# Third phase of a decoder step: output projection as plain fp32 matmuls of whole values in place of three products of high and low parts

## The chip, the cores and the metric

The kernel runs on one core of one Trainium2 chip. The time is the device time of the whole program in microseconds; of the kernel before there are three runs, median 2069.62 us (2069.22 to 2070.6). Times inside the program come from one profiled execution. Its span, from the first to the last instruction, is 2068.6 us, and its own time is 2070.4 us, 1.8 us more.

## The reference

One layer of a decoder with two parallel branches (latent attention and causal pooling), gated, merged, projected and added to the input, then a final norm. All is fp32; there are 2048 prompt tokens and 8 decoded ones. The change is in the last lines:

```python
merged = jax.nn.sigmoid(g_att) * y_att + jax.nn.sigmoid(g_pool) * y_pool
x = x + merged @ w_out                    # (2056 x 1024) @ (1024 x 1024)
...
y_prompt = rmsnorm(xp, g_final)
y_sample = rmsnorm(xs, g_final)
```

## The kernel before, in words

The program is one stream of instructions for each engine, tied by semaphores. First come the latent projections and attention, then the part called `merge`, whose tiles begin with `d_` in the profile. It has three phases. Phase one makes the gates (tiles `d_wr` with `d_ht` or `d_hb`), phase two the two branch projections and their gated sum (`d_wr` with `d_gat` or `d_gpl`; the sum is stored as `out_mg`), phase three multiplies the sum by `w_out`.

Nearly every large product is made of **high and low parts**. ScalarE copies an fp32 tile into one of type fp32r, which rounds it (the high part). VectorE subtracts that from the source (`split`, L91 to L93; the profile puts it down to L93) and has the low part, also fp32r. `three_products` (L127 to L134, the matmul is on L131) then issues three matmuls for each slice k of the contraction: high by high, high by low, low by high.

Phase three splits `w_out` and each group of 256 tokens into two by two quarters and uses a scheme of seven products in place of eight (Strassen's, in the form with 15 additions). Its moving operands are the seven quarters or sums of quarters of the weights, 28 tiles `moved[m]` of 128 x 2 x 512 (parts, columns); its stationary ones are the seven of the tokens, `kept[g % 2][k][part]`, 128 x 7 x 128 each. The quarters are staged in `d_staged` (loads on SP's queue, L2041 to L2052; sums on GpSimd, L2433 to L2444), and split by ScalarE (L2270) and VectorE (`low_staged`, L2542). The weights are split by L2255, L2260 and L2532 to L2540; the last ten of the 28 come late, as `d_raw`.

The order of work is the table `JOIN` (L1750 to L1764). A step (g, p) is product p of group g: four slices k, accumulated in one bank of PSUM over 512 columns. There are 8 groups x 7 products = 56 steps, in the order (0,1) (0,2) (0,6) (0,5) (0,7) and then for each group g: (g,1) (g-1,4) (g-1,3) (g,2) (g,6) (g,5) (g,7). Two more steps with g = 8 are the eight decoded tokens (`tail_product`, L2761), with a stationary of 8 columns, 20 slices together. TensorE's step (g,1) waits for the split tokens of the group (`kept_ok`, L2784); after each step ScalarE copies or VectorE adds the result out of PSUM and counts up `evicted` or `added`. At the end come the sum of squares (ScalarE), the factor (GpSimd, `rms`), the scaling (VectorE) and the store.

Two places elsewhere in the kernel issue matmuls on tiles of type f32, that is, plain fp32 ones:

```python
for hh in range(4):        # L627, inside "for a in range(2)", "for k in range(KQ)": 16 calls
    head = 4 * a + hh
    mm = pe.matmul(ps_q[2 * a + k][:, hh * R:hh * R + R], wuq_t[:, head, k * P:k * P + P],
                   wuk_t[:, head, :], start=True, stop=True)
...
for s, j, to in columns(g):   # L1670, four calls, eight times in all: 32 calls
    pe.matmul(ps_s[n % 2][to, :], qd[:, 0, s, :], ckeys[:, n % 2, j, :], start=True, stop=False)
```

The second has stationaries of 32 columns that write to four different groups of 32 partitions (`to`). L1674, right behind it, is of the same kind with 256 moving columns; L1683 has a stationary of 128 columns and 8 moving ones.

Of the kernel before, what the change touches and what calls it, by code (L numbers as in the profile page):

```python
# [20 lines left out]
f32 = mybir.dt.float32  # L21
# [3 lines left out]
ACT = mybir.ActivationFunctionType  # L25
# [55 lines left out]
HD = KD // 2  # L81
# [45 lines left out]
def three_products(pe, out, stationary, moving, depth, first=True, last=True, again=False):  # L127

    for k in range(depth):
        for a, b in ((0, 0), (0, 1), (1, 0)):  # L130
            mm = pe.matmul(out, stationary(a, k), moving(b, k),  # L131
                           start=first and k == 0 and a + b == 0,
                           stop=last and k == depth - 1 and a == 1, skip_group_check=again)
    return mm  # L134
# [1633 lines left out]
MOVED_OF = {1: 0, 2: 1, 6: 2, 5: 3, 7: 4, 4: 5, 3: 6}  # L1768
KEPT_OF = {1: 0, 2: 1, 4: 2, 5: 3, 6: 4, 7: 5, 3: 6}
# [21 lines left out]
def merge(nc, io, keep, ahead):  # L1791
# [6 lines left out]
    with ExitStack() as ctx:  # L1798
        def at(first, name, shape, dt=f32):
            return nc.alloc_sbuf_tensor_at("d_" + name, shape, dt, offset=first)  # L1800

        def sem(name):
# [20 lines left out]
        first = where["scores"]  # L1823
# [3 lines left out]
        out = [at(out_at + n * row, f"out{n}", [P, TA]) for n in range(4)]  # L1827
# [36 lines left out]
        moved = [at(first, f"moved{n}", [P, 2, HALF], f32r) for n, first in enumerate(wide_at)]  # L1864
        quarters = at(wide_at[0], "quarters", [P, 4, HALF])
        changed = at(wide_at[2], "changed", [P, 4, HALF])
        moved_f = [at(where["gap"] + n * piece, f"moved_f{n}", [P, HALF]) for n in range(2)]
        raw_at = {m: t_at[0] + (n * piece if n < 3 else 8 * NH * T - (len(RAW_ORDER) - n) * piece)
                  for n, m in enumerate(RAW_ORDER)}
        raw = {m: at(first, f"raw{m}", [P, HALF]) for m, first in raw_at.items()}  # L1870
# [8 lines left out]
        kept = [[[at(kept_at[2 * i + a], f"kept0_{i}_{a}", [P, 7, P], f32r) for a in range(2)] for i in range(HD)],  # L1879
                [[at(t_at[0] + (2 * i + a) * 3584, f"kept1_{i}_{a}", [P, 7, P], f32r) for a in range(2)]  # L1880
                 for i in range(HD)]]
# [8 lines left out]
        tail_f = at(staged_at[1], "tail_f", [P, KD, TAIL_C])  # L1890
        tail = at(staged_at[1] + 256, "tail", [P, 2, KD, TAIL_C], f32r)
# [3 lines left out]
        w_in, w_hi, w_ok, unit_ok = ahead["w_in"], ahead["w_hi"], ahead["w_ok"], ahead["unit_ok"]  # L1895
# [56 lines left out]
        moved_hi, moved_ok, MOVED_HI, MOVED_OK = const_hi, const_lo, 2, 3  # L1952
        staged_in, STAGED_BASE = ol_in, OL_BASE + 16 * NC * NH // 2
        TURN_BASE = added_t + 4 * HD
        kept_hi, kept_ok, KEPT_BASE = ahead["h_hi"], h_ok, 3 * HD * NAP
# [45 lines left out]
        staged_row = lambda n: staged[n % (2 if n < HD else 3)]  # L2001
# [211 lines left out]
        def _(act):  # L2213
# [38 lines left out]
            def high_moved(m):  # L2252

                act.wait_ge(moved_in[m % 2], MOVED_BASE[m % 2] + 16 * (m // 2 + 1))
                act.activation(moved[m][:, 0, :], moved_f[m % 2][:, :], ACT.Copy).then_inc(moved_hi, 1)  # L2255

            def high_raw(m):

                act.wait_ge(raw_in, RAW_BASE + 16 * len(RAW_ORDER))
                act.activation(moved[m][:, 0, :], raw[m][:, :], ACT.Copy).then_inc(moved_hi, 1)  # L2260

            def high_staged(q, i):

                n = HD * q + i
                if n == 1:
                    act.wait_ge(gp_lo, NC)
                if n == HD:
                    act.wait_ge(moved_ok, MOVED_OK + NMOVED)
                act.wait_ge(t_ok, TURN_BASE + 4 * n + 4)
                act.activation(kept[q % 2][i][0][:, :, :], staged_row(n)[:, 1:8, :], ACT.Copy).then_inc(kept_hi, 1)  # L2270

            def squares(q):

                act.wait_ge(added, add_join[q, 3])
                if q >= 2:
                    act.wait_ge(rinv_ok, 3 * (q - 1))
                for t in range(2):
                    for part in range(2):
                        n = 4 * q + 2 * t + part
                        wait(act, ss_ok, n - 2)  # L2280
                        act.activation(bank[JUNK_BANK[n % 3]][:, :], y[q % 2][t][:, part * HALF:part * HALF + HALF], ACT.Square,
                                       accum_out=stat[:, q % 2, part, t:t + 1]).then_inc(ss_ok, 1)

            for s, (g, p) in enumerate(SLOTS):
# [22 lines left out]
                if p == 4 and g + 1 - POOLED in pool_groups:  # L2307
                    n = pool_at(g + 1 - POOLED)
# [34 lines left out]
            for n, (g, p) in enumerate(JOIN):  # L2343
                act.wait_ge(unit_ok, UNITS + n + 1)
                if g < GROUPS_C:
                    if p == 1:
                        act.wait_ge(*((added, add_join[g - 1, 7]) if g else (m_ok, NC * KD)))
                        act.activation(p1c[:, :], bank[A_BANK[g % 2]][:, :], ACT.Copy).then_inc(evicted, 1)
                    if p == 6:
                        if g:  # L2350
                            act.wait_ge(added, add_join[g - 1, 3])
                        act.activation(u2c[:, :], bank[A_BANK[g % 2]][:, :], ACT.Copy).then_inc(evicted, 1)
                    if p == 7:
                        act.wait_ge(added, add_join[g, 5])
                        act.activation(p1c[:, :], bank[A_BANK[g % 2]][:, :], ACT.Copy).then_inc(evicted, 1)
                for m in JOIN_RAW.get((g, p), ()):
                    high_raw(m)
                for i in JOIN_STAGED.get((g, p), ()):
                    high_staged(pair_of(g, p), i)
                if (g, p) == (GROUPS_C - 1, 6):  # L2360
                    act.wait_ge(staged_in[0], STAGED_BASE + 48 * HD * GROUPS_C // 2 + 16)
                    act.activation(tail[:, 0, :, :], tail_f[:, :, :], ACT.Copy).then_inc(kept_hi, 1)
                if p == 3:
                    squares(g)
            act.wait_ge(added, add_join[GROUPS_C, 2])
            act.wait_ge(rinv_ok, 3 * (GROUPS_C - 1))
            for part in range(2):
                n = 4 * GROUPS_C + part
# [322 lines left out]
        def _(pe):  # L2691
# [10 lines left out]
            for s, (g, p) in enumerate(SLOTS):  # L2702
# [20 lines left out]
                if p == 1 and g - POOL_MM in pool_groups:  # L2723
                    n, pg = pool_at(g - POOL_MM), (g - POOL_MM) % PAIRS
# [4 lines left out]
                    for part in range(2):  # L2729
                        mm = three_products(pe, bank[PM_BANK[part]][:, 0:HA], lambda a, _: wpl[:, a, pg, :],  # L2730
                                            lambda b, _: pool2[:, b, HA * part:HA * part + HA], 1)
# [29 lines left out]
            def tail_product(out, pairs):  # L2761

                for n, (k0, block_of) in enumerate(pairs):
                    mm = three_products(pe, out, lambda a, k: tail[:, a, k0 + k, :],
                                        lambda b, k: moved[HD * block_of + k][:, b, :], HD,
                                        first=n == 0, last=n == len(pairs) - 1)
                mm.then_inc(unit_ok, 1)

            pe.wait_ge(yp_ok, NC * KD)
# [1 line left out]
            for g, p in JOIN:  # L2771
                if g == GROUPS_C:
                    pe.wait_ge(kept_ok, KEPT_BASE + HD * GROUPS_C + 1)
                    if p == 1:
                        pe.wait_ge(added, add_join[GROUPS_C - 1, 2])
                        tail_product(bank[C_BANK][0:TAIL_C, :], ((0, MOVED_OF[1]), (HD, MOVED_OF[2])))
                    else:
                        pe.wait_ge(added, add_join[GROUPS_C - 2, 4])
                        tail_product(bank[A_BANK[0]][0:TAIL_C, :], ((0, MOVED_OF[1]), (0, MOVED_OF[5]), (HD, MOVED_OF[3])))
                    continue  # L2780
                if g == 0:
                    pe.wait_ge(moved_ok, MOVED_OK + {5: HD * MOVED_OF[5] + HD, 7: 18 + 5}.get(p, HD * MOVED_OF[p] + HD))
                if p == 1:
                    pe.wait_ge(kept_ok, KEPT_BASE + HD * g + HD)  # L2784
                    if g >= 2:
                        pe.wait_ge(added, add_join[g - 2, 4])
                if p == 2 and g:
                    pe.wait_ge(added, add_join[g - 1, 2])
                if p in (6, 7):
                    pe.wait_ge(evicted, evict_join[g, 1 if p == 6 else 6])  # L2790
                if p == 4:
                    pe.wait_ge(evicted, evict_join[g, 7])
                if p == 5 and g >= 2:
                    pe.wait_ge(added, add_join[g - 2, 3])
                if p == 3:
                    pe.wait_ge(added, add_join[g, 7])
                to = bank[C_BANK if p == 2 else (B_BANK if p in (5, 3) else A_BANK)[g % 2]][:, :]
                of = kept[g % 2]
                three_products(pe, to, lambda a, k: of[k][a][:, KEPT_OF[p], :],
                               lambda b, k: moved[HD * MOVED_OF[p] + k][:, b, :], HD, first=p in (1, 2, 5),  # L2800
                               again=p in (6, 7, 4, 3)).then_inc(unit_ok, 1)


def finish(outs):
# [184 lines left out]
```

## Time and profile before

| | us |
|---|---|
| median of three runs | 2069.62 |
| profiled execution, its own time | 2070.4 |
| its span | 2068.6 |
| TensorE matmul busy (97% of the span) | 2005.8 |
| VectorE busy | 1498.7 |
| ScalarE busy | 1124.5 |
| GpSimd busy | 523.7 |
| phase three on TensorE, first matmul to last end | 1885.24 to 2061.80 |

Busy time of an engine is the union of its instructions' spans. A matmul's span reaches from its start to its modelled end; the next one starts well before that, so the time that a matmul costs in a dense stretch is the distance from start to start, not the mean duration. It is read from a window: its length divided by the number of instructions that touch it. Weight loads (PEld) are recorded apart and run beside the matmuls. The granted clock is 1.00 at TensorE's upper level of 2.4 GHz and 0.50 at its lower of 1.2 GHz.

### The profile page before, as it was taken

The numbers are of one execution on the slowest core, as the hardware profiler recorded it, in microseconds if no ns is written. First come the engines' busy times: TensorE is split into PE (matmuls) and PEld (weight loads), VectorE is DVE, ScalarE is ACT, GpSimd is POOL, SyncE is SP. The second block draws the span as 40 slices with busy tenths as digits, with TensorE's granted clock in tenths as the row PEclk, the third lists the DMA queues.
The fourth block names the chain that finished last, engine by engine and source line by source line (L and its number), as shares of the span: only waits on it lengthen the run. The fifth ranks groups of instructions, "written<-read, shape, count | busy, mean of one in ns | idle before, by whom it ended". The sixth has DMA issues, their size and how long they took to land.

```text
span 2068.6 us, 37208 instructions
## 1 busy us (share of the span) xinstructions
PE 2005.8 (97%) x13077; PEld 1831.8 (89%) x13077; DVE 1498.7 (72%) x3208; ACT 1124.5 (54%) x2271; POOL 523.7 (25%) x647
## 2 busy tenths in 40 slices
PE   7999999999999999999999999999999989998998
PEld 6999888888888888699999999999999989997885
DVE  7786887887888776568668758767875777675554
ACT  4446765556555555556665665666564434442442
POOL 3444364333211010213004003101111331122451
PEclk9999999999999999999999999999999999999999
DMA  8876465344221032367776776786888988886452
GB/s 302 267 237 187 121 192 168 112 123 125 90 72 31 6 122 92 129 174 224 245 235 206 248 232 194 259 246 195 252 273 255 322 285 296 289 282 192 135 175 84
DMA packets 284249, 396.97 MB, mean 192 GB/s; under 512 B 34016, under 2 KB 152680, under 8 KB 283032
## 3 DMA queue, kind: packets, MB, share of 16 engines
q1 hardware_dynamic: 278272, 374.26, 58.2%
q0 software_dynamic: 2304, 12.58, 1.6%
q10 hardware_dynamic: 3488, 7.75, 1.2%
q8 instruction: 105, 1.72, 0.3%
q14 instruction: 80, 0.66, 0.1%
HBM read 295.77 MB, written 98.96 MB: 191 GB/s over the span
## 4 chain that ended last, share of the span: by engine, by line
PE 40%; DVE 7%; issue 3%; DMA 3%; ACT 2%; POOL 1%; SPq 1%; ACTq 0%; DVEq 0%; POOLq 0%
PE b_ps L131 40%; DVE d_wr L93 3%; ACT d_wr L1345 1%; DMA d_moved_f<-in_w_quarters 1%; DMA d_quarters<-in_w_quarters 1%; DVE d_pool L93 0%; DVE d_pooled L2594 0%; POOL d_ols L93 0%; DMA d_zsf<-out_zs 0%; DVE d_c L2579 0%; DMA d_olf<-out_olat 0%; DVE d_moved L93 0%; DVE d_gat L93 0%; DVE d_out L2508 0%; DMA d_raw<-in_w_quarters 0%
## 5 line engine op out<-in xcount | busy, mean ns | idle before, releaser
L93 DVE TENSOR_TENSOR d_wr<-d_ws,d_wr 128x512 fp32r<-128x512 f32 x568 | 429.4, 762 | 210.3 <-ACT d_wr L1345 204.2
L1345 ACT ACTIVATE d_wr<-d_ws 128x512 fp32r<-128x512 f32 x568 | 350.1, 628 | 247.7 <-PE b_ps L131 239.5
L131 PE MATMUL b_ps<-d_ht,d_wr 128*128 128x258 f32 x3072 | 398.7, 284 | 6.8 <-DVE d_wr L93 5.2
L131 PEld LDWEIGHTS b_ps<-d_ht,d_wr 128*128 128x128 f32 x3072 | 380.2, 189 | 13.4 <-DVE d_wr L93 12.0
L759 PE MATMUL b_ps<-kt,k_qs 128*128 128x512 f32 (+2 forms) x1520 | 337.8, 370 | 1.2 <-DVE b_p L1147 1.1
L131 PE MATMUL b_ps<-d_hb,d_wr 128*128 128x258 f32 x2304 | 302.7, 284 | 6.2 <-DVE d_wr L93 4.6
L759 PEld LDWEIGHTS b_ps<-kt,k_qs 128*128 128x128 f32 x1520 | 265.4, 188 | 48.5 <-DVE b_p L1147 3.9
L131 PEld LDWEIGHTS b_ps<-d_hb,d_wr 128*128 128x128 f32 x2304 | 287.4, 189 | 9.3 <-DVE d_wr L93 7.3
L1101 ACT ACTIVATE b_pt<-b_ps 128x512 fp32r<-128x512 f32 x272 | 158.3, 597 | 167.5 <-PE b_ps L1207 114.0
L93 DVE TENSOR_TENSOR b_pt<-b_ps,b_pt 128x512 fp32r<-128x512 f32 x272 | 182.9, 688 | 87.8 <-ACT b_pt L1101 86.4
L1207 PE MATMUL b_ps<-b_pt,kv 128*128 128x512 f32 x816 | 227.8, 407 | 0.0
L1094 ACT ACTIVATE b_p<-b_p,b_bias 128x1024 f32<-128x1024 f32 (+7 forms) x192 | 171.6, 896 | 60.0 <-DVE b_low L1154 59.1
L131 PE MATMUL b_ps<-d_gat,d_wr 128*128 128x412 f32 x960 | 184.8, 353 | 2.2 <-DVE d_wr L93 2.2
L131 PEld LDWEIGHTS b_ps<-d_gat,d_wr 128*128 128x128 f32 x960 | 181.7, 191 | 4.0 <-DVE d_wr L93 2.9
L131 PE MATMUL b_ps<-d_moved,d_kept 128*128 128x512 f32 x672 | 160.5, 401 | 7.9 <-DVE d_spf L2630 5.6
L1207 PEld LDWEIGHTS b_ps<-b_pt,kv 128*128 128x128 f32 x816 | 143.4, 189 | 24.2
L131 PEld LDWEIGHTS b_ps<-d_moved,d_kept 128*128 128x128 f32 x672 | 129.1, 192 | 39.1 <-DVE d_spf L2630 5.9
L93 POOL TENSOR_TENSOR k_qs<-k_qf,k_qs 128x512 fp32r<-128x512 f32 (+1 forms) x52 | 71.1, 1368 | 359.8 <-issue 203.2
L1198 PE MATMUL b_ps<-ident,b_p 128*128 128x128 f32 x1088 | 149.0, 273 | 3.3 <-DVE b_pt L93 1.6
L1198 PEld LDWEIGHTS b_ps<-ident,b_p 128*128 128x128 f32 x1088 | 128.4, 140 | 25.6 <-DVE b_pt L93 3.3
L1147 DVE TENSOR_SCALAR_CACHE_REDUCE b_p<-b_ps 128x512 f32<-128x512 f32 (+1 forms) x192 | 125.1, 668 | 14.7 <-PE b_ps L759 13.0
L1171 DVE TENSOR_SCALAR b_p<-b_p,b_inverse 128x1024 f32<-128x1024 f32 (+7 forms) x192 | 133.2, 716 | 0.7
(248 smaller groups left out, 2562.9 us busy)
## 6 DMA issues: line engine op xcount, KB each, us to landing
d_ws<-out_w_sums SPq DMA_DIRECT2D x256, 256.0 KB, 3.5
d_ws<-in_w_pairs SPq DMA_DIRECT2D x192, 256.0 KB, 3.1
d_ws<-in_w_last SPq DMA_DIRECT2D x120, 256.0 KB, 4.4
b_quarters<-in_w_pairs SPq DMA_DIRECT2D x16, 1024.0 KB, 8.1
out_w_sums<-b_sums SPq DMA_DIRECT2D x16, 1024.0 KB, 10.3
out_q<-a_qout SPq DMA_DIRECT2D x32, 384.0 KB, 4.0
d_hf<-out_ht SPq DMA_DIRECT2D x32, 258.0 KB, 3.4
out_zs<-d_out SPq DMA_DIRECT2D x32, 258.0 KB, 4.3
```

The costliest lines, as they stand in the source:

```text
L93: return e.tensor_tensor(low, source, high.bitcast(f32), ALU.subtract)
L131: mm = pe.matmul(out, stationary(a, k), moving(b, k), start=first and k == 0 and a + b == 0, stop=last and k == depth - 1 and a == 1, skip ...
L759: mm = pe.matmul(out, qs[:, a, h, :], keep["kt"][:, first:first + size, b, :], start=k == 0, stop=k == len(pairs) - 1)
L1094: act.activation(span, span, ACT.Exp, bias=bias[:, at:at + 1], scale=-1.0 if negated else SCALE, accum_out=total[:, at, part:part + 1]).th ...
L1101: act.activation(pt[n % NPT][:, 0, :], ps_t[n % NTB][:, :], ACT.Copy).then_inc(pt_hi, 1)
L1147: dve.tensor_scalar(out, inp, 1.0, None, ALU.mult, ALU.max, accum_out=top[:, at, c:c + 1]).then_inc(s_sb, 1)
L1171: dve.tensor_scalar(span, span, inverse[:, at:at + 1], None, ALU.mult).then_inc(p_ok, 1)
L1198: mm = pe.transpose(ps_t[n % NTB][:, h * P:h * P + P], weights(u, h, slice(j * P, j * P + P)), ident[:, :])
L1207: mm = pe.matmul(ps_o[u % 2][:, :], kv[:, j, a, :], pt[n % NPT][:, b, :], start=j == 0 and k == 0, stop=j == tiles(u) - 1 and k == 2)
L1345: act.activation(ahead["wr"][s % WR][:, 0, :, :], ahead["ws"][s % WS][:, :, :], ACT.Copy).then_inc(ahead["w_hi"], 1)
```

## The change

In phase three each slice k is one matmul on whole fp32 values instead of three on parts. The tiles keep their places and sizes: `moved[m][:, 0, :]`, `kept[..][0]` and `tail[:, 0]` are now written through `bitcast(f32)`, so that ScalarE's copy does not round, and read through `bitcast(f32)`. VectorE's subtractions, the semaphores and their counts, the loads and the order of the steps are as before; the low tiles are still written but no matmul reads them.

```diff
             def high_moved(m):
-                act.activation(moved[m][:, 0, :], moved_f[m % 2][:, :], ACT.Copy).then_inc(moved_hi, 1)
+                act.activation(moved[m][:, 0, :].bitcast(f32), moved_f[m % 2][:, :], ACT.Copy).then_inc(moved_hi, 1)
...
-                act.activation(kept[q % 2][i][0][:, :, :], staged_row(n)[:, 1:8, :], ACT.Copy).then_inc(kept_hi, 1)
+                act.activation(kept[q % 2][i][0][:, :, :].bitcast(f32), staged_row(n)[:, 1:8, :], ACT.Copy).then_inc(kept_hi, 1)
...
             def tail_product(out, pairs):
                 for n, (k0, block_of) in enumerate(pairs):
-                    mm = three_products(pe, out, lambda a, k: tail[:, a, k0 + k, :],
-                                        lambda b, k: moved[HD * block_of + k][:, b, :], HD,
-                                        first=n == 0, last=n == len(pairs) - 1)
+                    for k in range(HD):
+                        mm = pe.matmul(out, tail[:, 0, k0 + k, :].bitcast(f32),
+                                       moved[HD * block_of + k][:, 0, :].bitcast(f32), start=n == 0 and k == 0,
+                                       stop=n == len(pairs) - 1 and k == HD - 1)
...
-                three_products(pe, to, lambda a, k: of[k][a][:, KEPT_OF[p], :],
-                               lambda b, k: moved[HD * MOVED_OF[p] + k][:, b, :], HD, first=p in (1, 2, 5),
-                               again=p in (6, 7, 4, 3)).then_inc(unit_ok, 1)
+                for k in range(HD):
+                    mm = pe.matmul(to, of[k][0][:, KEPT_OF[p], :].bitcast(f32),
+                                   moved[HD * MOVED_OF[p] + k][:, 0, :].bitcast(f32), start=p in (1, 2, 5) and k == 0,
+                                   stop=k == HD - 1, skip_group_check=p in (6, 7, 4, 3))
+                mm.then_inc(unit_ok, 1)
```

TensorE's program in step (0,1), the first of phase three, before. The names are the moving tile and the stationary one; of `d_kept_k_part` the second number is 0 for the high and 1 for the low part:

```order
L131 MATMUL b_ps<-d_moved_13099,d_kept_0_0_13142 128x512 [waits d_const_lo,d_h_ok,d_ya_ok,d_yp_ok]
L131 MATMUL b_ps<-d_moved_13099,d_kept_0_0_13142 128x512
L131 MATMUL b_ps<-d_moved_13099,d_kept_0_1_13143 128x512
L131 MATMUL b_ps<-d_moved_13100,d_kept_1_0_13144 128x512 x2
L131 MATMUL b_ps<-d_moved_13100,d_kept_1_1_13145 128x512
L131 MATMUL b_ps<-d_moved_13101,d_kept_2_0_13146 128x512 x2
L131 MATMUL b_ps<-d_moved_13101,d_kept_2_1_13147 128x512
L131 MATMUL b_ps<-d_moved_13102,d_kept_3_0_13148 128x512 x2
L131 MATMUL b_ps<-d_moved_13102,d_kept_3_1_13149 128x512
```

The same place of the changed kernel, with steps (0,2) and (0,6) behind it:

```order
L2801 MATMUL b_ps<-d_moved_13099,d_kept_0_0_13142 128x512 [waits d_const_lo,d_h_ok,d_ya_ok,d_yp_ok]
L2801 MATMUL b_ps<-d_moved_13100,d_kept_1_0_13144 128x512
L2801 MATMUL b_ps<-d_moved_13101,d_kept_2_0_13146 128x512
L2801 MATMUL b_ps<-d_moved_13102,d_kept_3_0_13148 128x512
L2801 MATMUL b_ps<-d_moved_13103,d_kept_0_0_13142 128x512 [waits d_const_lo]
L2801 MATMUL b_ps<-d_moved_13104,d_kept_1_0_13144 128x512
L2801 MATMUL b_ps<-d_moved_13105,d_kept_2_0_13146 128x512
L2801 MATMUL b_ps<-d_moved_13106,d_kept_3_0_13148 128x512
L2801 MATMUL b_ps<-d_moved_13107,d_kept_0_0_13142 128x512 [waits d_evicted,d_const_lo]
```

Twelve matmuls became four, in the same order of slices and behind the same waits. The last step of the program, that of the decoded tokens, was 36 matmuls and is 12:

```order
L131 MATMUL b_ps<-d_moved_13099,d_tail 8x512 [waits d_added,d_h_ok]
L131 MATMUL b_ps<-d_moved_13099,d_tail 8x512 x2
L131 MATMUL b_ps<-d_moved_13100,d_tail 8x512 x3
L131 MATMUL b_ps<-d_moved_13101,d_tail 8x512 x3
L131 MATMUL b_ps<-d_moved_13102,d_tail 8x512 x3
```

```order
L2765 MATMUL b_ps<-d_moved_13099,d_tail 8x512 [waits d_added,d_h_ok]
L2765 MATMUL b_ps<-d_moved_13100,d_tail 8x512
L2765 MATMUL b_ps<-d_moved_13101,d_tail 8x512
L2765 MATMUL b_ps<-d_moved_13102,d_tail 8x512
L2765 MATMUL b_ps<-d_moved_13111,d_tail 8x512
```

What moved is only TensorE's own list; the rows of ScalarE, VectorE, GpSimd and SP are the same in both kernels. A row here is a call in the program, and the trace can hold more than one record for it.

## Rows read from the trace of the kernel before

**Rows 1.** The page: busy tenths and granted clock in 40 slices.
```profile
PE   7999999999999999999999999999999989998998
PEclk9999999999999999999999999999999999999999
```

**Rows 2.** Chain that ended last, from 1885 us: start us, us, what, count.
```profile
1885.24 5.50 PE b_ps L131 x12
...
1890.77 0.60 ACT d_p1c L2348
...
1895.52 1.10 DVE d_kept L93
1896.69 0.03 SPq L2047
...
1897.59 2.57 DMA d_staged<-out_mg
...
1902.10 0.96 ACT d_kept L2270
...
1903.15 1.10 DVE d_kept L93
...
1904.30 157.50 PE b_ps L131 x672
2061.80 0.78 issue
...
2065.10 1.27 DVE d_y_tail L2687
```

**Rows 3.** Windows, matmuls of L131: stretch, length, PE and PEld busy (touching), clock.
```profile
1885.00:1890.97 5.97, 5.73 (x14) 4.47 (x15) 0.50 0.54 133
1890.97:1904.30 13.33, 11.04 (x48) 8.65 (x46) 1.00 0.76 233
1904.30:1908.00 3.70, 3.70 (x9) 2.94 (x10) 0.54 0.62 190
1925.00:2050.00 125.00, 125.00 (x541) 99.00 (x540) 1.00 0.45 143
```

**Rows 4.** Window, all engines: PE, PEld, DVE, ACT, POOL busy, PE clock.
```profile
1925.00:1950.00 25.00, 25.00 (x109) 20.23 (x108) 15.49 (x18) 9.05 (x17) 14.11 (x26) 1.00 0.58 182
```

**Rows 5.** Groups of TensorE by form: busy us, mean ns | idle before, releasers.
```profile
L131 PE MATMUL b_ps<-d_moved,d_kept 128*128 128x512 f32 x672 | 160.5, 401 | 7.9 <-DVE d_spf L2630 5.6 <-DVE d_kept L93 2.3
L131 PE MATMUL b_ps<-d_moved,d_tail 128*8 128x512 f32 x60 | 14.2, 394 | 0.0
L131 PEld LDWEIGHTS b_ps<-d_moved,d_kept 128*128 128x128 f32 x672 | 129.1, 192 | 39.1 <-DVE d_spf L2630 5.9 <-DVE d_kept L93 2.7
```

**Rows 6.** Plain fp32 matmuls by line: duration ns min/median/max, first and last start us.
```profile
L629 PE MATMUL b_ps<-a_wuk_t,a_wuq_t x32: 275/421/582, 8.1 to 14.3; 128*128 128x128 f32 x32
L1671 PE MATMUL b_ps<-c_ckeys,e_qd x64: 588/593/617, 832.0 to 871.8; 128*32 128x512 f32 x64
L1674 PE MATMUL b_ps<-c_rkeys,e_qd x128: 377/379/380, 832.9 to 872.8; 128*32 128x256 f32 x128
L1683 PEld LDWEIGHTS b_ps<-kt,e_qd x16: 190/192/193, 829.4 to 831.1; 128*128 128x128 f32 x16
L1683 PE MATMUL b_ps<-kt,e_qd x16: 175/256/257, 829.5 to 831.1; 128*128 128x8 f32 x16
```

**Rows 7.** Timeline of TensorE in three short windows near 842 us: start, us, what.
```profile
841.76 0.64 PE L1671 MATMUL b_ps<-c_ckeys,e_qd 128*32 128x512 f32 x4
842.22 0.61 PE L1671 MATMUL b_ps<-c_ckeys,e_qd 128*32 128x512 f32 x4
842.64 0.40 PE L1674 MATMUL b_ps<-c_rkeys,e_qd 128*32 128x256 f32 x4
```

**Rows 8.** L629 after 14 us, the part at the upper clock.
```profile
L629 PE MATMUL b_ps<-a_wuk_t,a_wuq_t x6: 275/275/276, 13.7 to 14.3; 128*128 128x128 f32 x6
```

**Rows 9.** Groups of ScalarE that write fp32r and f32: busy us, mean ns.
```profile
L1101 ACT ACTIVATE b_pt<-b_ps 128x512 fp32r<-128x512 f32 x272 | 158.3, 597 | 167.5 <-PE b_ps L1207 114.0 <-PE b_ps L1198 47.7 <-issue 2.2
L2352 ACT ACTIVATE d_u2c<-b_ps 128x512 f32<-128x512 f32 x8 | 4.8, 596 | 3.6 <-PE b_ps L131 3.6
```

More of the change, by code:

```diff
@@ L2254, in high_moved @@
                 act.wait_ge(moved_in[m % 2], MOVED_BASE[m % 2] + 16 * (m // 2 + 1))
-                act.activation(moved[m][:, 0, :], moved_f[m % 2][:, :], ACT.Copy).then_inc(moved_hi, 1)
+                act.activation(moved[m][:, 0, :].bitcast(f32), moved_f[m % 2][:, :], ACT.Copy).then_inc(moved_hi, 1)
             def high_raw(m):
                 act.wait_ge(raw_in, RAW_BASE + 16 * len(RAW_ORDER))
-                act.activation(moved[m][:, 0, :], raw[m][:, :], ACT.Copy).then_inc(moved_hi, 1)
+                act.activation(moved[m][:, 0, :].bitcast(f32), raw[m][:, :], ACT.Copy).then_inc(moved_hi, 1)
             def high_staged(q, i):
@@ L2361, in _ @@
                     act.wait_ge(staged_in[0], STAGED_BASE + 48 * HD * GROUPS_C // 2 + 16)
-                    act.activation(tail[:, 0, :, :], tail_f[:, :, :], ACT.Copy).then_inc(kept_hi, 1)
+                    act.activation(tail[:, 0, :, :].bitcast(f32), tail_f[:, :, :], ACT.Copy).then_inc(kept_hi, 1)
                 if p == 3:
```

## The prediction, made before the changed kernel was run

> **What bounds the kernel now.** I read the page first: TensorE is busy nine tenths or more in nearly every slice and at its upper clock [rows 1]. So a change in TensorE's work shows in the time one to one, if the place that it touches is as dense as the rest. The chain of waits answers that for phase three [rows 2]: from 1904.30 to 2061.80 us it is nothing but matmuls of L131, 157.50 us for 672 of them, and before that it goes once through TensorE (12 matmuls, 5.50 us) and once around it, through the tokens of group 1. The idle time says the same: 5.6 us before the first matmul, 2.3 us before step (1,1), none else [rows 5]. The other engines have room: in a window of 25 us VectorE is busy 15.49, ScalarE 9.05, GpSimd 14.11 [rows 4]. The end behind the last matmul, 6.8 us (2061.80 to 2068.6), is squares, factor and scaling of the decoded tokens, and is not touched.
>
> **The change, part by part.**
>
> *Removed:* 672 + 60 = 732 matmuls on parts [rows 5]. Their cost is the distance from start to start, not the 401 ns of the group row. In the window 1925 to 2050, 541 touch 125.00 us at clock 1.00 [rows 3]; with the last one's duration of about 0.39 added, 125.39 / 541 = 231.8 ns. The pure column time would be 512 / 2.4 GHz = 213 ns, so each bears some 18 ns of surcharge. The chain agrees: (157.50 - 1.6 for a piece at the lower clock - 0.2) / 672 = 231.7.
>
> *Added:* 56 x 4 + 20 = 244 calls on whole values. Three things must be known of one: how many records it is, how long each holds TensorE, and whether the weight load hides.
> Records: L629 stands in the program as 16 calls and L1671 as 32, and the trace has 32 and 64 [rows 6]. So a plain fp32 call is two matmuls, and 244 calls are 488 records.
> Time of one: L1671 has our 512 columns, L1674 256, both at the upper clock; their durations are 593 and 379 [rows 6]. The difference, 214 ns for 256 columns, is 0.836 ns a column, two cycles of 2.4 GHz; 512 columns are 428 ns. The starts agree: four L1671 at 841.76 (side by side, in four column groups), their second records at 842.22, L1674 at 842.64 [rows 7], steps of 0.46 and 0.42, 0.44 in the mean. These stationaries are 32 columns wide and ours are 128. For that there is L629 with 128: six records from 13.7 to 14.3 at duration 275 [rows 8], about 0.11 apart for 128 columns, again two cycles a column with at most a few ns on top. So I take 0.430 us a record, 0.860 a call, against 3 x 0.2318 = 0.695 before. Bounds: 0.42 from below (the shortest step of the row); from above 2 x 0.2318 = 0.464, if each of the two cycles per column bears the surcharge of a whole pass before.
> Weight loads: 192 ns for 128 columns of plain fp32, by L1683 [rows 6], as for the parts [rows 5]. Each would lie beside a matmul of 430, where it now lies beside one of 232. I cost it at nothing. If it were not covered, L1683, whose 8 columns hide nothing, prices it: 16 records from 829.5 to 831.1, 0.107 each.
>
> The Trainium skill has a rule here, in "FP8 and Floating Point Precision", TensorE Precision Notes: true FP32 takes four passes through the array. By column time alone four passes are 4 x 213 = 853 ns a call, which is what the two records of two cycles a column give; the trace would show them folded in pairs. Read as four passes each as dear as one before, it gives the upper bound above, and is a rival below.
>
> *The start of the phase.* Here something is given back. Before, the clock was at 0.50 until 1890.97 [rows 3], after the idle 5.6 us; it should be again, since nothing ahead of 1885.24 changes. Plain records then take 0.86: (1890.97 - 1885.24) / 0.86 = 6.7 of them by the time the clock rises. Step (0,1) has 8, so the last starts at about 1891.1 and ends at 1891.7, where it ended at 1890.74 before. The first five steps are 40 records: 33.3 more at 0.43 is 14.3 us, and TensorE is ready for step (1,1) at 1905.3. What it waits for there are the split tokens of group 1. Their chain starts at the end of step (0,1): ScalarE's copy, the last weights, VectorE's splits, SP's load, 2.57 us of transfer, sums, ScalarE, VectorE, ready at 1904.26 [rows 2]. It starts 1.0 us later, so it ends at 1905.3. Both arrive together: the idle time that ended at 1904.30 is used up by slower matmuls, and step (1,1) starts 1.0 us later, not 6. Without the idle time there is also no fall to clock 0.50: before, the first 3.4 us after 1904.30 ran at half speed (0.54 in the row [rows 3]; 9 matmuls touch 3.70 us), about 1.6 us lost, which this sum doesn't have.
>
> *The rest.* 732 - 60 = 672 matmuls before, 488 - 40 = 448 records after: 448 x 0.430 = 192.6 us. The last one's end comes 0.16 after its slot (593 - 430 ns). 1905.3 + 192.6 + 0.2 = 2098.1 against 2061.80, **+36.3 us**. The gross sum, 488 x 0.430 - 732 x 0.2318 = 209.8 - 169.7 = +40.1, less the idle time (2.4) and the fall of the clock (1.6), is 36.1, the same but for the longer use of the lower clock at the start.
>
> *What costs nothing.* ScalarE's copies write f32 where they wrote fp32r: a PSUM copy of 512 columns took 596 and 597 ns in the two types [rows 9]. VectorE still subtracts, as long as before, though the result is read by none; in this phase it is covered by TensorE. Evictions come at the same points of longer steps, so each gets more time (a step was 12 x 0.232 = 2.8 us and becomes 3.4). SP's loads and stores hang on the steps and move along with them. No wait is added.
>
> **Rivals.**
> 1. *Not slower: a record of the whole-value product takes one cycle a column.* Place: each of 488 records; price 0.232 instead of 0.430. Then 488 x 0.232 = 113 us, 56 less than before, about 2013. It decides below (169.7 + 4) / 488 = 0.356 us a record. For it: no row has 128 stationary and 512 moving columns in plain fp32. Against it: both shapes at hand say two cycles.
> 2. *The surcharge comes along.* The 18 ns above column time may belong to reading 512 fp32 columns and not to the type. Once per record: 448 x 0.0185 = +8, 2114. Twice, the upper bound of 0.464: 448 x 0.034 = +15, 2121. For it: every shape of parts shows it. Against it: the L1671 and L1674 rows show 214 ns per 256 columns, none of it.
> 3. *The idle time and the fall of the clock stay.* If the tokens of group 1 are later than I think (their chain passes ScalarE and VectorE steps that wait for TensorE's steps), 2.3 us of idle time and 1.7 of lower clock come back: 2110.
> 4. *The weight load shows.* 448 x 0.107 = +48, 2154. For it: two loads per call, each after the other. Against it: 192 against 430 ns. The Trainium skill speaks for it ("TensorE: Matmul & The Clock Gate", Weight-path perf modes): fast weight load is off for FP32. The rows do not show a slower load, 192 ns in both types.
>
> **How the numbers follow.** The forecast has 0.77, rival 1 has 0.01, rival 2 has 0.09 (0.06 once, 0.03 twice), rival 3 has 0.11, rival 4 has 0.02. The profiled execution gives 2070.4 + 36.3 = 2106.7, its own time lying 0.8 above the median of the runs; on the median of 2069.62 it is 2105.9. I say 2106. The range: a record of 0.4235, half-way to the lower bound, takes off 2.9, so 2103; above it takes in rival 3 and the first form of rival 2, 2114. About 0.2% (4 us) is what a measurement of this kernel can tell from no change; the forecast and rivals 2 to 4 are all far above it, rival 1 alone is below. Slower 0.98, and of the rest half each for faster and same (a price between the two).
>
> **What the changed profile would show.** The group of phase three with 448 records in place of 672, and 40 in place of 60, mean duration near 593; a window in mid-phase with some 291 per 125 us (0.430 each); weight loads still near 192 and beside the matmuls; idle time before the group only the 5.6 us at its start; clock 1.00 throughout after 1891; TensorE's last end near 2098. I am wrong if there is one record per call, if records stand 0.45 or more apart, if idle time appears between steps, or if VectorE or ScalarE ends the chain in mid-phase.

## The result and the profile after

| | before | after |
|---|---|---|
| median of three runs, us | 2069.62 | 2107.05 (2104.59 to 2111.57) |
| ratio to before, 95% interval | | 1.0183 (1.0155 to 1.0211) |
| five more runs, beside nine of before | 2070.42 | 2108.01; ratio 1.0174 (1.0161 to 1.0188) |
| span of the profiled execution | 2068.6 | 2105.2 |
| TensorE matmul busy | 2005.8 | 2044.1 |

The change costs 37 us, 1.8%. I forecast 2106, 36 more than before.

First the chain of waits of the changed kernel (start, us, what, count), which answers to [rows 2]:

```profile
1892.67 2.49 DVE d_moved L93 x3
...
1896.17 1.10 DVE d_kept L93
...
1898.25 3.12 DMA d_staged<-out_mg
...
1903.29 0.96 ACT d_kept L2270
...
1904.34 1.10 DVE d_kept L93
...
1905.49 168.50 PE b_ps L2801 x392
2073.99 6.96 PE b_ps L2765 x16
2080.95 7.07 PE b_ps L2801 x16
2088.01 10.41 PE b_ps L2765 x24
2098.43 0.78 issue
...
2101.73 1.27 DVE d_y_tail L2687
```

The shape is that of before: one way around TensorE through the tokens of group 1, then matmuls to the end, now from 1905.49 to 2098.43 where it was 1904.30 to 2061.80. The four pieces of TensorE hold 392 + 16 + 16 + 24 = 448 records in 192.94 us. What follows the last matmul takes 6.8 us, as before.

The groups of TensorE and its weight loads (busy us, mean ns | idle before, releasers), which answer to [rows 5]:

```profile
L2801 PE MATMUL b_ps<-d_moved,d_kept 128*128 128x512 f32 x448 | 196.0, 600 | 6.2 <-DVE d_spf L2630 5.9 <-DVE d_kept L93 0.3
L2765 PE MATMUL b_ps<-d_moved,d_tail 128*8 128x512 f32 x40 | 17.5, 592 | 0.0
L2801 PEld LDWEIGHTS b_ps<-d_moved,d_kept 128*128 128x128 f32 x448 | 86.0, 192 | 115.8 <-issue 108.4 <-DVE d_spf L2630 6.2 <-DVE d_kept L93 1.2
```

224 calls of L2801 are 448 records and 20 of L2765 are 40. The matmul's duration rose from 401 to 600 ns, and the weight load stayed at 192. The loads now have 108 us of idle time, in which they wait for nothing but their turn. The 2.3 us that TensorE waited for the tokens are 0.3.

Windows of L2801 (length, PE and PEld busy with the number that touch it, granted clock), which answer to [rows 3]:

```profile
1885.00:1890.97 5.97, 5.97 (x8) 2.48 (x9) 0.52 0.58 140
1890.97:1904.30 13.33, 13.33 (x33) 5.92 (x32) 1.00 0.68 209
1904.30:1908.00 3.70, 3.36 (x8) 1.27 (x8) 1.00 0.64 151
1925.00:2050.00 125.00, 125.00 (x293) 55.38 (x292) 1.00 0.41 126
```

(125.00 + 0.59) / 293 = 0.4286 us a record against 0.2318. A count of touching records can be off by one in 293; from the first to the last start in the window the trace has 0.4292 a record, against 0.2316 before. The chain gives 192.94 / 448 = 0.431: it also holds the end of the last record, and behind its first record and at each change between L2801 and L2765 the distance is some 0.1 us longer. In the row of 1904.30 the clock is at 1.00, where it was 0.54: it no longer falls.

The other engines did the same work in more time. Window of all engines, which answers to [rows 4]:

```profile
1925.00:1950.00 25.00, 25.00 (x60) 11.12 (x59) 12.36 (x14) 7.83 (x16) 8.88 (x20) 1.00 0.42 127
```

VectorE is at 12.36 of 25 us, after 15.49.

### The profile page after: what moved, and what is told of

The parts are those of the page before. It is cut to its first block, busy times and chain, and to the rows that moved or that the text cites. A ratio compares the mean times of both kernels' runs of the same rounds, so it can differ in the third digit from the quotient of the medians.

```text
span 2105.2 us, 36720 instructions
## 1 busy us (share of the span) xinstructions
PE 2044.1 (97%) x12833; PEld 1785.9 (85%) x12833; DVE 1498.1 (71%) x3208; ACT 1125.1 (53%) x2271; POOL 516.7 (25%) x647
## 4 chain that ended last, share of the span: by engine, by line
PE 40%; DVE 9%; issue 3%; DMA 2%; ACT 2%; SPq 1%; POOL 1%; ACTq 0%; DVEq 0%; POOLq 0%
PE b_ps L131 31%; PE b_ps L2801 8%; DVE d_wr L93 3%; ACT d_wr L1345 1%; PE b_ps L2765 1%; DMA d_moved_f<-out_w_moved 1%; DVE d_gat L93 0%; DVE d_pool L93 0%; DVE d_saf L2636 0%; DVE d_spf L2630 0%; DVE d_pooled L2594 0%; DVE d_c L2579 0%; DMA d_quarters<-in_w_quarters 0%; DMA d_moved_f<-in_w_quarters 0%; DVE d_ht L93 0%
## 5 line engine op out<-in xcount | busy, mean ns | idle before, releaser
L131 PE MATMUL b_ps<-d_ht,d_wr 128*128 128x258 f32 x3072 | 398.7, 284 | 6.9 <-DVE d_wr L93 5.4
L131 PEld LDWEIGHTS b_ps<-d_ht,d_wr 128*128 128x128 f32 x3072 | 380.1, 189 | 13.5 <-DVE d_wr L93 12.4
L131 PE MATMUL b_ps<-d_hb,d_wr 128*128 128x258 f32 x2304 | 302.8, 284 | 6.2 <-DVE d_wr L93 4.6
L131 PEld LDWEIGHTS b_ps<-d_hb,d_wr 128*128 128x128 f32 x2304 | 287.5, 189 | 9.3 <-DVE d_wr L93 7.2
L2801 PE MATMUL b_ps<-d_moved,d_kept 128*128 128x512 f32 x448 | 196.0, 600 | 6.2 <-DVE d_spf L2630 5.9
L131 PE MATMUL b_ps<-d_gat,d_wr 128*128 128x412 f32 x960 | 185.7, 354 | 2.5 <-DVE d_wr L93 2.5
L131 PEld LDWEIGHTS b_ps<-d_gat,d_wr 128*128 128x128 f32 x960 | 182.3, 191 | 4.6 <-DVE d_wr L93 3.6
L2801 PEld LDWEIGHTS b_ps<-d_moved,d_kept 128*128 128x128 f32 x448 | 86.0, 192 | 115.8 <-issue 108.4
```

The lines of the kernel that those rows point to most:

```text
L131: mm = pe.matmul(out, stationary(a, k), moving(b, k), start=first and k == 0 and a + b == 0, stop=last and k == depth - 1 and a == 1, skip ...
L2801: mm = pe.matmul(to, of[k][0][:, KEPT_OF[p], :].bitcast(f32), moved[HD * MOVED_OF[p] + k][:, 0, :].bitcast(f32), start=p in (1, 2, 5) and ...
```

## The experiments

Eight kernels ran. Each was timed beside the kernel before. Differences are of medians where nothing else is said; the kernel before had 2070.42 beside the first four (nine runs) and 2071.55 beside the last four (thirteen), which ran on another chip. So across the two groups the ratios to the kernel before are what to compare.

**e1_again: the changed kernel once more.** No edit.

> The changed kernel once more, five rounds, since its first three runs lay 7 us apart (2104.6 to 2111.6) where the kernel before had 1.4. Theory (the cost is matmul time in a phase where TensorE never waits): median within 2104 to 2110, about 37 us over the kernel before, ratio near 1.018, and the profile again 488 records 0.429 us apart. If the spread is chance in an earlier part of the program, it shows in the kernel before as well when that has more runs. Rival (the slower step pace itself makes the runs unsteady): the changed kernel spreads over 5 us or more again, the kernel before under 2.

Measured: 2108.01 (2105.31 to 2109.29), ratio 1.0174 (1.0161 to 1.0188). The nine runs of before went from 2068.45 to 2074.57, so they spread as far as the changed one (2104.59 to 2111.57 in all eight). The rival is out. The first matmul of the phase stood at 1884.8 in the first profile, at 1887.6 in this one and at 1888.3 in that of e2, with the same work ahead of it; so some us of the spread are made earlier in the program. From there to the last matmul's end the same kernel took 213.6 us in its first profile and 211.8 in this one: here the lower clock lasted some 3.7 us in place of some 6, and TensorE did not wait before step (1,1) at all.

**e2_rounded: plain products on rounded values.** ScalarE writes fp32r as before, only the matmuls are plain:

```diff
-                act.activation(moved[m][:, 0, :].bitcast(f32), moved_f[m % 2][:, :], ACT.Copy).then_inc(moved_hi, 1)
+                act.activation(moved[m][:, 0, :], moved_f[m % 2][:, :], ACT.Copy).then_inc(moved_hi, 1)
```

and so for the other three copies.

> Only the products are changed: plain fp32 matmuls as in the changed kernel, but on tiles that ScalarE still writes as fp32r, so on rounded values with empty low bits (the output lacks what the low parts carry). Theory (the type of the matmul sets its time, not what ScalarE wrote): the same as the changed kernel within 0.2%, 2107, records 0.429 us apart. Rival (ScalarE's copy to f32 or the values in the low bits cost or save something): off by more than 4 us.

Measured: 2108.93, ratio 1.018 (1.0165 to 1.0196), 0.9 above e1. A window of the same 125 us holds 292 records:

```profile
1925.00:2050.00 125.00, 125.00 (x292) 55.34 (x291) 59.58 (x67) 40.65 (x77) 46.47 (x102) 1.00 0.41 126
```

The type in which the matmul reads its operands sets the time; the type of ScalarE's copy and the low bits of the values do not, within the noise of a us or two.

**e3_two_products: as many records as the changed kernel, of parts.** The kernel before without the product of the stationary's low part in phase three:

```diff
-        for a, b in ((0, 0), (0, 1), (1, 0)):
+        for a, b in parts:          # phase three passes ((0, 0), (0, 1)), all others the three
```

> The kernel before with two products of parts instead of three in phase three (the product of the stationary's low part is left out), so 488 records of 512 columns, exactly as many as in the changed kernel, on high-part tiles. Theory (one cycle a column for parts, two for plain values): each record 0.232 us, phase three from 1885.2 to about 2006, time about 2014, 56 below the kernel before and 93 below the changed one, with TensorE still without idle time. Rival A (a record costs the same whatever its type, and the count matters): about 2105. Rival B (the phase is close to another limit, the making of the token parts): over 2025, with idle time before steps (g,1).

Measured: 2048.02, ratio 0.9885 (0.987 to 0.9901), 22 below before and 60 below the changed kernel at the same number of records. So the count is not what costs (rival A is out), but my 2014 failed too, and rival B holds. The group of phase three, busy, mean | idle:

```profile
L131 PE MATMUL b_ps<-d_moved,d_kept 128*128 128x512 f32 x448 | 115.3, 415 | 29.9 <-DVE d_kept L93 15.6 <-DVE d_spf L2630 5.5 <-ACT d_u2c L2352 5.3
```

TensorE now waits, for the tokens above all: behind its first matmul the phase has 24.4 us of idle time where it had 2.3. From the first matmul to the last end it takes 148.8 us (1888.96 to 2037.75) after 176.6, so only 28 of the 56 us that were taken away come back there; 22 of the rest are idle time, and some 6 went into a lower clock (0.94 in the mean) and the ends of matmuls before each wait, which this run does not tell apart. Of the 28, six are lost again outside: this profile's phase starts 3.7 us later, and what follows the last matmul takes 2.4 longer. The chain of this kernel shows a loop that returns after 17.17 us (17.2 to 17.6 from group to group in mid-phase):

```profile
1964.01 2.14 PE b_ps L131 x8
...
1966.18 0.70 DVE d_u2c L2674
...
1966.90 0.69 DVE d_y L2676
1967.60 1.01 DVE d_kept L93
...
1969.58 2.24 DMA d_staged<-out_mg
...
1974.17 0.96 ACT d_kept L2270
...
1978.25 1.48 DVE d_y L2559
...
1981.18 2.14 PE b_ps L131 x8
```

One step of TensorE lets VectorE add its result; behind that in VectorE's queue stands the token split that frees a staging tile; then follow load, GpSimd's sums, ScalarE's and VectorE's split, and VectorE's scaling and sums ahead of TensorE's next step. In the kernel before TensorE needs 84 x 0.232 = 19.5 us a group; in the changed one 56 x 0.429 = 24.0. The loop holds one step of TensorE, 8 records here and 12 in the kernel before; with the four more, 0.9 us, it would return there every 18.1 to 18.5 us. That is an estimate from this chain, and by it TensorE's bound is only 1.0 to 1.4 us a group longer than the loop.

**e4_halves: every plain call cut into two of 256 columns.** Twice the records and weight loads for the same columns:

```diff
                 for k in range(HD):
-                    mm = pe.matmul(to, of[k][0][:, KEPT_OF[p], :].bitcast(f32),
-                                   moved[HD * MOVED_OF[p] + k][:, 0, :].bitcast(f32), start=p in (1, 2, 5) and k == 0,
-                                   stop=k == HD - 1, skip_group_check=p in (6, 7, 4, 3))
+                    for c in (slice(0, 256), slice(256, 512)):
+                        mm = pe.matmul(to[:, c], of[k][0][:, KEPT_OF[p], :].bitcast(f32),
+                                       moved[HD * MOVED_OF[p] + k][:, 0, c].bitcast(f32),
+                                       start=p in (1, 2, 5) and k == 0 and c.start == 0,
+                                       stop=k == HD - 1, skip_group_check=p in (6, 7, 4, 3) or c.start > 0)
```

> The changed kernel with each plain call cut into two of 256 columns, so 976 records and 976 weight loads for the same columns; the work is the same. Theory (two cycles a column, weight loads of 0.192 us wholly beside the matmuls): a record takes 0.2145 to 0.216 us, the phase 0 to 2 us longer, time about 2108. Rival (the weight load is a second limit, partly in the open): every added load shows up to 0.107 us, 488 x 0.107 = 52 us, time up to 2159.

Measured: 2107.44, ratio 1.018 (1.0164 to 1.0195), 0.6 below e1, within the noise. Window of L2804, the same line in this kernel:

```profile
1925.00:2050.00 125.00, 125.00 (x581) 110.04 (x580) 1.00 0.42 128
```

(125.00 + 0.38) / 581 = 215.8 ns a record. Twice the weight loads (busy 110 of 125 us) cost no more than 2.5 ns a record: they lie beside the matmuls. Rival 4 of the prediction is out.

**e5_thin_lows: the changed kernel almost without VectorE's subtractions.**

```diff
-                split(dve, moved[m][:, 1, :], moved_f[m % 2][:, :], moved[m][:, 0, :]).then_inc(moved_ok, 1)
+                split(dve, moved[m][:, 1, 0:8], moved_f[m % 2][:, 0:8], moved[m][:, 0, 0:8]).then_inc(moved_ok, 1)
```

Likewise for the last weights, and two of 128 columns for the tokens.

> The changed kernel with VectorE's subtractions for phase three cut to a sliver (8 of 512 columns for the weights, 2 of 128 for the tokens), since no matmul reads the low tiles; about 53 us of VectorE work goes (28 at 0.75, 32 at 1.10). Theory (TensorE alone sets the end, VectorE is covered): the stretch from the first to the last matmul is the same but for the remaining 0.5 us of idle time before step (1,1), and the first matmul may start 1 to 2 us earlier, since the splits of the last weights stand ahead of the last sum of phase two; time 0.5 to 3 us below the changed kernel, 2105 to 2108. Rival (the low parts' making is a real part of the 37 us): 10 us or more below it.

Measured: 2104.48, ratio 1.0162 (1.0145 to 1.0179). By ratios that is 2.5 us below e1 (by medians, of two chips, 3.5); the intervals overlap, so only a few us at most are there. VectorE is 41.40 us busy in the 125 us window, after 61.61 in the changed kernel, and 293 records touch it, as there:

```profile
1925.00:2050.00 125.00, 125.00 (x293) 55.47 (x292) 41.40 (x67) 39.45 (x77) 41.37 (x95) 1.00 0.42 131
```

TensorE's group:

```profile
L2801 PE MATMUL b_ps<-d_moved,d_kept 128*128 128x512 f32 x448 | 194.5, 597 | 4.0 <-DVE d_spf L2630 4.0
```

What gain there is lies ahead of the phase: the idle time before it is 4.0 us where it was 5.9 and, in e1, 5.3. None is left before step (1,1), but e1 had none there either, and from the first matmul to the last end both take 211.8 us. The subtractions fell from 53.9 to 11.2 us of VectorE's time, 43 us less where I had expected 53, and 20 of them in this window; the phase gave back nothing for it.

**e6_one_product and e7_one_thin: where the other engines bound the phase.** e6 is e3 with `parts=((0, 0),)`, high by high alone; e7 is e6 with the subtractions cut as in e5.

> The kernel before with only the product of high by high in phase three (both products with low parts are left out): 244 records at 0.232 us. Theory (below about 17 us a group the phase is bound not by TensorE but by the tokens: VectorE's two sums and a split, load, GpSimd's sums, ScalarE's and VectorE's split, and the loop closes through one step of TensorE): of the 57 us of TensorE work taken away from the run with two products little comes back, some 1.2 us a group and 11 at the end of the phase, time 2022 to 2032, groups about 16 us apart. Rival (TensorE still sets most of it): 2048 - 57 = 1991.

> As the run with high by high alone, and VectorE's subtractions for phase three cut to slivers as well. Theory (the loop of the tokens bounds it, and holds two token splits of 1.0 to 1.1 us a group): about 2 us a group and 2 us at the start less than the run with one product, 12 to 18 us in all. Rival (those splits are beside the loop): within 4 us of it.

Measured: e6 2040.41 (ratio 0.9853, 0.9836 to 0.9869), 7 below e3 by ratios and 8 above my range's upper end; e7 2023.85 (0.9772, 0.9754 to 0.9789), 16.6 below e6, as forecast. From e6's timeline of TensorE, the pieces that begin with step (g,1) in three groups in a row (start, us, what, count, idle before):

```profile
1934.26 3.78 PE L131 MATMUL b_ps<-d_moved,d_kept 128*128 128x512 f32 x8 [3.39 <-DVE d_kept L93]
...
1950.68 3.78 PE L131 MATMUL b_ps<-d_moved,d_kept 128*128 128x512 f32 x8 [3.33 <-DVE d_kept L93]
...
1967.95 3.78 PE L131 MATMUL b_ps<-d_moved,d_kept 128*128 128x512 f32 x8 [3.31 <-DVE d_kept L93]
```

and the whole phase in one window of e6 (PE, PEld, DVE, ACT, POOL, clock):

```profile
1885.00:2023.00 138.00, 83.53 (x244) 55.80 (x242) 92.78 (x107) 59.51 (x117) 82.01 (x133) 0.73 0.55 173
```

The groups are 16.4 to 17.3 us apart, where I had 16. The granted clock is 0.73 in the mean, with TensorE idle for up to 3.4 us at a time, and it reaches into the loop. If the loop runs as in e3, its step of TensorE is the first four records of these two pieces:

```profile
1939.24 3.98 PE L131 MATMUL b_ps<-d_moved,d_kept 128*128 128x512 f32 x16 [1.20 <-DVE d_y L2670]
...
1955.67 5.35 PE L131 MATMUL b_ps<-d_moved,d_kept 128*128 128x512 f32 x16 [1.20 <-DVE d_y L2670]
```

In the first the clock is at 1.00 and the step takes 1.2 us, where e3's eight records took 2.1; that group is 16.4 us long. In the second the clock is at 0.50 for the 2.1 us that the same step takes, and the group is 17.3 us long, as in e3. The other groups go the same way, 16.4 to 16.7 us with that step at clock 1.00 and 17.3 with it at 0.50. So where the clock is down, TensorE's shorter step gives the loop nothing. With thin splits (e7) the period is 15.0 to 15.5 us, the last one 16.2.

**e8_parts_halves: every product of parts cut into two of 256 columns.**

```diff
+        for a, b in ((0, 0), (0, 1), (1, 0)):
+            for c in (slice(0, 256), slice(256, 512)):
+                mm = pe.matmul(out[:, c], stationary(a, k), moving(b, k)[:, c],
+                               start=first and k == 0 and a + b == 0 and c.start == 0,
```

> The kernel before with each product of parts in phase three cut into two of 256 columns: 1464 records for the same columns. It asks whether the 18 ns by which a record of 512 columns exceeds its 213 ns of column time belongs to the record or to the columns. Theory (mostly to the columns: 412 columns stood 188 to 190 ns apart and 258 about 120, so 0.44 ns a column and 6 a record): 0.119 us a record, 1464 x 0.119 = 174 against 170, time 3 to 6 us above the kernel before. Rival (18 ns a record): 0.125 us, 183, 13 us above. If plain and parts are split alike, plain ones, where 256 columns stood 0.2155 apart, show the other pattern: no surcharge by column.

Measured: 2074.97 in ten runs, ratio 1.0016 (1.0006 to 1.0025), 3.4 above before. The window:

```profile
1925.00:2050.00 125.00, 125.00 (x1055) 124.52 (x1054) 1.00 0.46 144
```

(125.00 + 0.28) / 1055 = 118.7 ns for 256 columns, against 231.8 for 512: 0.442 ns a column and 5.6 a record. For plain values the starts in the traces of e4 and the changed kernel are 215.8 and 429.2 apart, 0.833 ns a column and 2.5 a record. The surcharge of the parts belongs for the most part to the columns, 6% over the 0.417 ns of one cycle; plain values, at two cycles, don't bear it. The weight loads are not its cause: they are busy 110 of 125 us in e4, which has no surcharge, and 99 in the kernel before, which has. Whether part of the 5.6 ns is theirs isn't shown, for in this run they are busy 124.52 of 125 us.

## Why the prediction was right

- **Records per call, two.** Right: 448 and 40, as the 16 and 32 calls of L629 and L1671 had shown.
- **Time of a record, 0.430 us.** Measured 0.4286 by the window and 0.4292 from start to start. The four column groups of L1671 and the 128 columns of L629 were together the right witnesses for a shape that no row of before had. Rival 1 (one cycle a column) and rival 2 (the surcharge comes along, 0.4485 or 0.464) are out by that number; e4 and e8 show that plain values lack what each column of the parts bears.
- **Weight loads at nothing.** Right, 192 ns beside 429. e4 shows that there was room for twice as many. The price of rival 4 was read from rounded starts: the records of L1683 stand 0.112 apart, so it would have been +50 and not +48.
- **The start.** I had step (1,1) at 1905.3, it was 1905.49; the idle time that would be used up is 0.3 us in place of 2.3, and the clock did not fall, so rival 3 is out. The mechanism is as forecast, but that it met the time within 0.2 us is in part luck. The first matmul came 0.4 us earlier than before (1884.81 for 1885.24), and that point lies anywhere from 1881.5 to 1889.0 in the profiles of the runs shown. ScalarE's copy behind step (0,1), where the chain of the tokens starts, came 0.7 us later (1891.45 for 1890.77), and the transfer took 3.12 us for 2.57, so the tokens were ready 1.2 us later; TensorE was ready at 1905.15.
- **The rest, 448 x 0.430 = 192.6.** Measured 192.94. End of TensorE 2098.43 for 2098.1, end of the program 2105.2 for 2104.9. In e1 the same kernel's TensorE ended at 2099.43, and over the larger sets of runs the change is 37.6 us where I had 36.3. The lower end of my range has a slip: half-way from 0.430 to the bound of 0.42 is 0.425, so 2104 and not 2103; the result lies inside either way.
- **What costs nothing.** ScalarE's copies: shown by e2. VectorE's subtractions on unused low parts: e5 puts them at some 3 us, within the noise, of which 1.3 to 1.9 can be seen as shorter idle time before the phase, where the splits of the last weights stand ahead of the last sum of phase two in VectorE's queue. It doesn't touch the forecast of the change, as they stand in both kernels.

What the prediction didn't see, since nothing hung on it: by its rows of idle time TensorE looked like the only bound of phase three, and e3 shows a second one 1.0 to 1.4 us a group behind, by the estimate above. For a change that makes TensorE slower it plays no part. For one that makes it faster it takes most: of the 56 us that two products save, 28 came in the phase and 22 in the time.

The three products of parts remain the faster form, 3 x 232 = 695 ns against 858. Only a run with less of the computation (e3, e6, e7) was faster than before. The change still made low parts that nobody reads; without most of them (e5) it is still 33 us slower than before. That plain values would also need no copy of ScalarE's was not tried.

## What to carry to other kernels

A matmul on plain fp32 tiles costs two records of two cycles a column, 858 ns for 512 columns, so where TensorE is the bound it would pay only against four products of parts or more (4 x 232 = 928, an estimate); against three it loses 23%. Where the other engines are the bound, what plain values spare them counts: between e6 and e7 the subtractions were worth 16.6 us, in the changed kernel some 3. Price a new shape from start-to-start distances of the nearest rows, once for the columns and once for the width of the stationary, and not from mean durations, which reach beyond the next start (600 ns beside 429 here). Before taking work off an engine that never waits, look for the loop that would bound it next: its period in e3 was 88 to 90% of TensorE's 19.5 us.

## What the runs showed of the hardware

- fp32r streams take 6% more than one cycle a column, and not evenly. In the kernel before, 22 matmuls in a row from 1953.5 us lasted 389 ns each, and eleven from 1958.9 on 392 to 402, with the same shape and clock; plain ones are 592 to 593 throughout such a stretch. From start to start the mean of a step is 226.7 to 234.6 ns, and the pattern comes back every 14 steps, that is two groups, to 0.2 ns. So it goes with the place in the program, such as the tiles read or the bank written, and is no chance. What sets it stays open; no run tried that. The kernel before (duration ns min/median/max, first and last start):

```profile
L131 PE MATMUL b_ps<-d_moved,d_kept x22: 389/389/390, 1953.5 to 1958.3; 128*128 128x512 f32 x22
L131 PE MATMUL b_ps<-d_moved,d_kept x11: 392/396/402, 1958.9 to 1961.3; 128*128 128x512 f32 x11
```

The changed kernel in the same stretch:

```profile
L2801 PE MATMUL b_ps<-d_moved,d_kept x22: 592/593/593, 1952.8 to 1961.8; 128*128 128x512 f32 x22
```

- In e6, where TensorE is idle for 1.2 to 3.4 us several times a group, the granted clock is 0.73 in the mean; in e3, with fewer and shorter gaps, 0.94. Part of what a kernel gains by doing less on TensorE goes back that way: in e6 a step of four records took 1.2 us at clock 1.00 and 2.1 at 0.50.
